# Alternating the two head pairs in the stick-breaking stage of a hybrid encoder layer on one Trainium2 core

## What is computed

```
def stick_breaking_attention(q, k, v):
    ...
        z = jnp.einsum('bhqd,bhkd->bhqk', qi, kf).astype(jnp.float32) * scale
        ...
        before = kpos[None, :] < qpos[:, None]
        log_beta = jax.nn.log_sigmoid(z)
        log_1m = jnp.where(before, jax.nn.log_sigmoid(-z), 0.0)
        tail = lax.cumsum(log_1m, axis=3, reverse=True) - log_1m
        w = jnp.where(before, jnp.exp(log_beta + tail), 0.0)
        return jnp.einsum('bhqk,bhkd->bhqd', w.astype(vf.dtype), vf)
```

```
    mixed = jnp.concatenate(
        [rms_norm(o_a, ga), rms_norm(o_b, gb), rms_norm(o_c, gc)], axis=-1)
    y = jnp.einsum('bse,ed->bsd', mixed, w_out[l])
```

## Time and profile before

| | us |
|---|---|
| median of three runs | 1052.81 |
| the runs | 1053.06, 1050.79, 1052.81 |
| the profiled execution | 1052.49 |
| its span (first to last instruction) | 1050.8 |
| PE busy in it | 1009.5 (96%) |
| DVE busy | 801.1 (76%) |
| ACT busy | 568.5 (54%) |

### The profile page before, as it was taken

The page is one execution under the profiler, slowest core; times in us unless marked ns, Lnnn a source line. Parts: engine busy times, 40 slices in busy tenths (PEclk is TensorE's granted clock), DMA queues, the critical chain, the costliest instruction groups (busy, mean ns, idle before and its releaser), DMA issues.

```text
span 1050.8 us, 12384 instructions
## 1 busy us (share of the span) xinstructions
PE 1009.5 (96%) x4940; PEld 816.1 (78%) x4940; DVE 801.1 (76%) x752; ACT 568.5 (54%) x747; POOL 92.4 (9%) x71
## 2 busy tenths in 40 slices
PE   7999999998999999999999999999999999999992
PEld 5878777886767787788788888788888788888782
DVE  6247659698577579977878867998777998768998
ACT  7423532658758536677653557343666434565453
POOL 0013213121312143000000000000000000000000
PEclk9999999999989999999999999999999999999997
DMA  9421111200001544013013022031031031043003
GB/s 327 140 71 41 41 41 41 80 1 2 23 20 41 203 155 164 1 41 120 1 49 112 1 89 72 1 101 60 1 120 41 1 120 41 1 163 158 1 0 160
DMA packets 38656, 74.64 MB, mean 71 GB/s; under 512 B 3236, under 2 KB 12744, under 8 KB 38600
## 3 DMA queue, kind: packets, MB, share of 16 engines
q1 hardware_dynamic: 38600, 73.86, 20.3%
HBM read 65.46 MB, written 8.39 MB: 70 GB/s over the span
## 4 chain that ended last, share of the span: by engine, by line
PE 89%; DVE 6%; ACT 2%; issue 2%; DMA 0%; SPq 0%; ACTq 0%; DVEq 0%
PE ps L700 27%; PE ps L702 27%; PE ps L704 27%; PE ps L911 2%; PE ps L865 2%; PE ps L936 1%; PE ps L769 1%; DVE out_gained L2038 1%; DVE y L1991 1%; DVE a_op L1937 1%; DVE y L2097 1%; ACT sb_w L1291 1%; PE ps L800 1%; ACT sb_r L1287 0%; DVE b_op L1948 0%
## 5 line engine op out<-in xcount | busy, mean ns | idle before, releaser
L700 PE MATMUL ps<-a_op,b_op 128*128 128x512 f32 x448 | 175.5, 392 | 4.0 <-issue 1.3
L700 PE MATMUL ps<-b_op,a_op 128*128 128x512 f32 x448 | 174.7, 390 | 3.6 <-issue 3.6
L704 PE MATMUL ps<-a_op,b_op 128*128 128x512 f32 x448 | 174.4, 389 | 0.0
L702 PE MATMUL ps<-a_op,b_op 128*128 128x512 f32 x448 | 174.3, 389 | 0.0
L704 PE MATMUL ps<-b_op,a_op 128*128 128x512 f32 x448 | 174.3, 389 | 0.0
L702 PE MATMUL ps<-b_op,a_op 128*128 128x512 f32 x448 | 174.3, 389 | 0.0
L700 PE MATMUL ps<-act_hi,w_hi 128*128 128x512 f32 x288 | 115.4, 401 | 7.2 <-DVE act_lo L1633 7.2
L1445 ACT CAST a_op<-f 128x1024 fp32r<-128x1024 f32 x56 | 58.8, 1050 | 112.9 <-PE ps L704 72.8
L1948 DVE TENSOR_TENSOR b_op<-wq,b_op 128x1024 fp32r<-128x1024 f32 x96 | 117.1, 1219 | 0.0
L702 PE MATMUL ps<-act_lo,w_hi 128*128 128x512 f32 x288 | 113.0, 392 | 0.0
L704 PE MATMUL ps<-act_hi,w_lo 128*128 128x512 f32 x288 | 112.8, 392 | 0.0
(11 more groups left out here) (216 smaller groups left out, 1672.2 us busy)
## 6 DMA issues: line engine op xcount, KB each, us to landing
wq<-in_w_ff_in SPq DMA_DIRECT2D x16, 1024.0 KB, 5.3
wq<-in_w_ff_out SPq DMA_DIRECT2D x16, 1024.0 KB, 5.1
stage<-in_w_in SPq DMA_DIRECT2D x16, 512.0 KB, 4.6
y<-in_x SPq DMA_DIRECT2D x4, 1024.0 KB, 12.5
stage<-in_w_out SPq DMA_DIRECT2D x8, 512.0 KB, 4.2
h_spill<-y SPq DMA_DIRECT2D x8, 512.0 KB, 2.7
h_back<-h_spill SPq DMA_DIRECT2D x2, 2048.0 KB, 11.7
out<-y SPq DMA_DIRECT2D x8, 512.0 KB, 2.7
```

Of the source, the lines that this page charges most:

```text
L700: nc.tensor.matmul(dst, stat[0], mov[0], start=first, stop=False, skip_group_check=chained)
L702: nc.tensor.matmul(dst, stat[0], mov[1], start=False, stop=False, skip_group_check=chained)
L704: return nc.tensor.matmul(dst, stat[1], mov[0], start=False, stop=last, skip_group_check=chained)
```

## The change

`UNITS` now goes through the query tiles in the outer loop and the pairs in the inner one: both pairs at t = 7, both at t = 6, down to both at t = 0. Before, pair 0 went from t = 7 down to t = 0, and then pair 1.

The rows are dealt out by halves. `FILL` lists places (u, a) that get half a row: both places in units 0 to 3 and 12 to 15, the first place alone in units 4 to 11. That is again 24 halves, 12 rows. A row whose halves stand in two units ends in the second one, and ACT copies it at the next head (`row_ends`). `SUM_UNIT` goes from 6 to 5, and with it `group_sums`, `group_variance` and POOL's `sum_squares`. Bank 6 now holds two tiles of both pairs when it is full, so that `output_copy` is two copies of half the width (`o_copied` counts to 8). `SPLIT_HEADS` and `MIX_HEADS` stay.

```
-        UNITS = [(p, t) for p in range(2) for t in reversed(range(TOK))]
+        UNITS = [(p, t) for t in reversed(range(TOK)) for p in range(2)]
...
-        FILL_UNITS = (0, 1, 2, 3, 4, 5, 8, 9, 10, 11, 12, 13)
-        N_EARLY = WINDOW_ROWS + len(FILL_UNITS)
-        SUM_UNIT, SPLIT_HEADS = 6, (7, 21)
+        FILL = tuple((u, a) for u in range(len(UNITS)) for a in range(2)
+                     if a == 0 or u < 4 or u >= 12)
+        N_EARLY = WINDOW_ROWS + len(FILL) // 2
+        SUM_UNIT, SPLIT_HEADS = 5, (7, 21)
         MIX_HEADS = (17, 19)
-        def row_of(u):
-            return WINDOW_ROWS + FILL_UNITS.index(u)
+        def half_rows(u, a):
+            for row, half in (divmod(i, 2) for i, place in enumerate(FILL) if place == (u, a)):
+                yield WINDOW_ROWS + row, range(2 * half, 2 * half + 2)
+        def row_ends(n):
+            for i, (u, a) in enumerate(FILL):
+                if i % 2 and 2 * u + a == n - 1:
+                    yield WINDOW_ROWS + i // 2
+        SUM_ROW = WINDOW_ROWS + sum(i % 2 and u <= SUM_UNIT for i, (u, a) in enumerate(FILL))
+        def out_cols(u):
+            p, t = UNITS[u]
+            return slice(P * (2 * (t % 2) + p), P * (2 * (t % 2) + p + 1))
...
             for u in range(len(UNITS)):
                 head_turn(2 * u)
                 if u:
                     weighted(u - 1)
-                if u in FILL_UNITS:
-                    recurrent_out(row_of(u), range(2))
+                for row, ks in half_rows(u, 0):
+                    recurrent_out(row, ks)
                 if u + 2 < len(UNITS):
                     scores(u + 2)
                 head_turn(2 * u + 1)
-                if u in FILL_UNITS:
-                    recurrent_out(row_of(u), range(2, OUT_K))
+                for row, ks in half_rows(u, 1):
+                    recurrent_out(row, ks)
...
             def output_copy(chain):
-                p, half = chain // 2, 1 - chain % 2
+                t = UNITS[CHAIN * (chain + 1) - 1][1]
                 act.wait_ge(pv_done, CHAIN * (chain + 1))
-                nc.scalar.copy(o_t[p][:, BANK * half:BANK * (half + 1)], ps[:, 6, :])\
-                    .then_inc(o_copied, 1)
+                both = ps[:, 6, :].rearrange("p (t a q) -> p a t q", t=2, a=2)
+                for p in range(2):
+                    nc.scalar.copy(o_t[p][:, P * t:P * (t + 2)].rearrange("p (t q) -> p t q", t=2),
+                                   both[:, p]).then_inc(o_copied, 1)
...
             for n in range(HEADS):
                 u, a = divmod(n, 2)
-                if a == 0 and u - 1 in FILL_UNITS:
-                    recurrent_row(row_of(u - 1))
+                for row in row_ends(n):
+                    recurrent_row(row)
                 if n + LEAD < HEADS:
                     weights(n + LEAD)
                 turned_copies(n)
```

More of the change, by code:

```diff
@@ L932, in weighted @@
                 elif u % CHAIN == 0:
-                    pe.wait_ge(o_copied, u // CHAIN)
+                    pe.wait_ge(o_copied, 2 * (u // CHAIN))
                 for j in range(t + 1):
@@ L936, in weighted @@
                         mm = nc.tensor.matmul(
-                            ps[HEAD * a:HEAD * (a + 1), 6, P * (t % 4):P * (t % 4 + 1)],
+                            ps[HEAD * a:HEAD * (a + 1), 6, out_cols(u)],
                             vtok[:, j, P * p + HEAD * a:P * p + HEAD * (a + 1)],
@@ L954, in recurrent_out @@
                     pe.wait_ge(row_copied, n)
-                    if n == row_of(FILL_UNITS[6]):
+                    if n == SUM_ROW:
                         pe.wait_ge(grp_var, 2)
@@ L990, in _ @@
                 head_turn(2 * u + 1)
-                if u in FILL_UNITS:
-                    recurrent_out(row_of(u), range(2, OUT_K))
+                for row, ks in half_rows(u, 1):
+                    recurrent_out(row, ks)
                 if u == SUM_UNIT:
-                    pe.wait_ge(row_copied, row_of(FILL_UNITS[6]))
+                    pe.wait_ge(row_copied, SUM_ROW)
                     group_sums(1, 7, win_sq[:, 0, :])
@@ L1020, in _ @@
                 if e == 0:
-                    pe.wait_ge(o_copied, 4)
+                    pe.wait_ge(o_copied, 8)
                 if s == 0:
@@ L1359, in _ @@
                     nc.scalar.preload_act_table_set("natural_log_exp_and_others")
+            for row in row_ends(HEADS):
+                recurrent_row(row)
             output_copy(len(UNITS) // CHAIN - 1)
             group_rsqrt(1)
-            act.wait_ge(o_copied, 4)
+            act.wait_ge(o_copied, 8)
             for k in range(2):
```

## The result

The changed kernel takes 1055.02 us (median of five runs, 1054.79 to 1056.16), the kernel before 1050.79 (1049.94 to 1053.06) on the same chip. The ratio is 1.0035, with an interval from 1.002 to 1.005: slower by 3.7 us by the ratio, where 1050.8 and a range to 1053.6 were forecast. The profiled execution took 1054.86 us (span 1053.1), 2.37 more than the one profiled before. The stage of the change holds most of this: from the first `head_turn` to the first row behind the loop it takes 356.21 - 256.65 = 99.56 us, before 353.84 - 255.99 = 97.85. Behind the stage nothing differs (697 us in both). The other 0.66 us stand ahead of the first `head_turn`: 0.22 is `scores(1)`, one block longer, and 0.42 lies ahead of anything that the change touches.

What follows compares the result with a forecast made beforehand. The prediction took PE as the bound of the stage. From the profiled 1052.49 us, new waits of 6.15 against 9.5 that go gave -3.35, and a clock fall +1.7: 1050.8 us, range 1047.7 to 1053.6.

Steps and rivals of the forecast that it cites:

- What PE's steps cost: Prices of PE's steps from unit 1; claimed the change adds and removes no matmul, so only waits differ.
- The sum: Over the whole stage: new waits of 6.15 us against 9.5 us that go, giving -3.35 us.
- start: Heads 2 and 3 grow to 1024 keys: longer scores(1) and longer ACT reads of z, +0.6 us.
- first split: At heads 7 and 8: PE waits 0.5 us for a row copy, 0.65 for head 9, 2.1 for head 10; 3.25.
- second split: Split with heads of 256 keys behind it: PE waits 1.5 us, against at most 0.2 before.
- Its own sign for the seam: In the changed kernel's profile, PE's timeline between units 7 and 8 has no wait over 0.3 us.
- the things that it named as showing it wrong: No wait at heads 9 and 10, clock low over 10 us, or ACT or DVE gapless through units 0 to 3.
- A fall was forecast at the first split: One short fall of the clock behind the first split's stall, costing 1.7 us; chance 0.45.
- The seam's loss: Between the two head pairs before the change: 6.3 us lost, 6.05 of it from 302.00 to 312.24; all goes.
- the end of the loop: Units 12 to 15: waits for ACT's copies of finished rows, 0.8 us in all, for the 2.25 that go.
- The fall given back in full: Rival: clock low at the split as long as at the seam, costing 4.2 us, 1053.3; chance 0.13.
- the slower one: Rival: low clock feeds itself from the split until group_sums passes in unit 5, costing 7.3 us, 1056.4; chance 0.09.

## Why the prediction was wrong

**The step that failed** is the sum itself, under "What PE's steps cost" and "The sum". It says that only waits differ, and lists the places of new waits as start, first split, second split and end: 6.15 us. Units 6 to 10 between the splits carry no term, which means that their bare second places were priced at nothing. They cost 4.8 us. Its own sign for the seam failed on this: it allowed no wait over 0.3 us between units 7 and 8, and 1.06 stands there (318.04, above); but none of the things that it named as showing it wrong came, because none concerned the units behind the split. The rows to see it were there: in the earlier trace rows half a row stands from 268.82 to 270.29 between the second transposition (268.08) and the next unit's first, and in the earlier trace rows ACT needs 1.08 us for two copies and 0.69 for a read. The prediction used just this count for unit 4, where it added the split, and did not carry it on to the units behind, where the half row is missing as well. That the reads ahead of the copy are the smaller part, it could not see from these rows; the run with the copies first showed that.

**The clock of the changed kernel.** A fall was forecast at the first split, for 1.7 us. The profiled execution has none: from 290 to 300 us PE is busy for 7.40 of 10 us and the clock reads 1.00. Four of its five runs have a mean clock of 0.992; the fifth has 0.990 and took 1056.16, 1.2 us more than the median of the others. So the size was about right, as far as one run tells, and the chance too high. The Trainium skill ("TensorE: Matmul & The Clock Gate", section "A second HAM failure mode: psum-queue depth-cycling") reports of another kernel that such pauses made the clock swing. In this trace, with 2.85 us of pauses at the split, they did not.

The prediction had also misread the seam's clock: it set the 1.15 us of waiting ahead of the fall. That wait ends at 303.56, so it began at 302.41, and the clock stood at 0.50 from 302.00; in the 6 us ahead of the fall PE was idle for 0.25 us.

**The seam's loss.** The 6.3 us are right for the profiled execution of before. But 4.2 of them were put down to the slow clock, and by the mean clock not every run has it. Of the 70 runs of the kernel before beside the experiments, on three chips, 41 have a mean clock of 0.988 or 0.989, median 1052.98 us, and 28 have 0.991 to 0.993, median 1049.71. The gain from a removed fall is thus about 3.3 us and exists in six runs of ten. The three runs shown before, 1050.79 to 1053.06, lie in the range of both kinds.

**The other terms held.** The start was put at 0.6 us and the timeline shows 0.59. The first split was put at 0.5 + 0.65 + 2.1 = 3.25; it shows 0.25, 0.58 and, by starts, 2.02, together 2.85. The second split was put at 1.5 and cost 1.1 by starts (0.77 in the brackets), the end of the loop at 0.8 and shows 0.08 + 0.55 + 0.41 = 1.0. Of what was costed at nothing, the copy of row 13 and the moved sums of squares show no wait on PE.

**The sum, corrected**, between executions at full clock: the waits that go are 9.5 - 4.2 = 5.3 us, the new ones 0.6 + 2.85 + 4.8 + 1.1 + 1.0 = 10.35, so +5.05 us. The runs give 1054.94 (median of the four runs of the change at 0.992) - 1049.71 = +5.2. That the two agree so closely is partly luck: with the 3.3 us that the runs give for the slow clock the waits that go are 6.2 and the sum is +4.15, and the runs stand on different chips. Against the profiled execution of before the same waits give 10.35 - 9.5 = +0.85 us where 2.37 were measured. Of the difference 0.42 lies ahead of the change (above), 0.9 would be explained if the slow work at the seam cost only what the runs show, and 0.2 is not assigned.

**The rivals.** "The fall given back in full" (1053.3) and the slower one (1056.4) named times on either side of the result, and the slower side, where it fell, was put at 0.11. Both came there by the clock, which stayed full, so that their nearness is luck. What came true, ACT's copies as a new wait in the units between the splits, was not among the rivals.

## What to carry to other kernels

When work that covers waits is dealt out anew, list every place that loses its cover, and for each the round trip through the other engine that becomes visible there: the end of the last product, what stands ahead on that engine's queue, its own duration, and the way back. One place costed so and five like it left at nothing made this prediction wrong; five of the 24 halves in better places turned +3.7 us into -0.5, and with more halves moved and VectorE's two rests later it became -4.1. And before a slow clock is booked as a loss that can be removed, look whether all runs have it.

## What the runs showed of the hardware that was not expected

By their mean clock, the runs of one and the same kernel have a stretch at 1.2 GHz of differing length or none, and their times go with it: two groups with medians 3.3 us apart (41 and 28 of 70 runs, above). Only one execution of the kernel before was profiled, one with the long stretch. Where the profiled executions showed such a stretch in the stage, it took 10.24 us in that of before and 3.40 to 3.42 us in those of five other kernels.

A fall also came with no wait of PE's ahead of it. In the kernel with whole rows in units 0 to 5, PE was busy for every microsecond of the 15 before; the windows of that execution:

```profile
292.00:302.36 10.36, 10.36 (x76) 7.58 (x75) 7.43 (x7) 7.51 (x17) 2.59 (x4) 1.00 0.31 103
302.36:307.63 5.27, 5.27 (x52) 4.16 (x52) 1.19 (x2) 2.71 (x7) 0.29 (x1) 1.00 0.00 0
307.63:311.04 3.41, 3.41 (x12) 2.72 (x11) 3.34 (x4) 2.60 (x6) 0.64 (x2) 0.50 0.01 2
```

In the middle stretch, beside products and transpositions, stand the group sums, 16 passes of one column each:

```profile
304.46 1.95 PE L796 MATMUL ps<-ones,win_sq 128*128 128x1 f32 x16
```

The changed kernel had the same sums in its stage, and 2.85 us of waits at the split, and in its profiled execution kept the clock at 1.00. Which work or pause decides was not settled.
